# Attention scores by pairs of query tiles, with the low keys' product on 64 of the array's 128 rows

## The chip, the cores and the metric

The kernel runs on one core of one Trainium2 chip. The metric is the device time of one execution in microseconds (us), as the median of several runs. TensorE is called PE below, its weight loads PEld, VectorE DVE, ScalarE ACT, GpSimd POOL; the queues that issue their DMAs have a q behind the name.

## The reference

One layer of a hybrid decoder, with 2048 prompt rows and 8 sample rows. The change is inside branch A, causal attention over the prompt with 8 heads of width 64 and a decay term in the logits:

```python
def block(i):                       # 128 queries at a time, i = 0 .. 15
    qb = lax.dynamic_slice_in_dim(q, i * 128, 128, axis=1)
    cq = lax.dynamic_slice_in_dim(c, i * 128, 128, axis=2)
    sc = einsum('bqhd,bkhd->bhqk', qb, k) * 64 ** -0.5 + cq[..., None] - c[:, :, None, :]
    sc = where(kpos <= qpos, sc, -inf)
    p = softmax(sc, axis=-1)
    return einsum('bhqk,bkhd->bqhd', p, v)
```

The other branches (a gated recurrence, and cross-attention into 256 memory tokens), the input projection of 1024 columns into all of them, and the merge are left as they are.

## The kernel before

The program is a chain of stages on one core: the input rows are normalised and projected (to 903 us), the recurrence runs (925 to 1337 us), then the attention of branch A in `attend_prompt` (scores from 1382.7 to 2168.7 us), the memory attention (from 2218.4 us), and the merge, to 2859 us. PE works through the remaining columns of the input projection in the recurrence and both attentions: `fill` hands it a fixed number of such products at fixed places (L2683, 128x512 each), so that PE has work while other engines prepare the next attention step. How many there are, and where, is dealt out ahead by `fill.deal`, not by time.

All products keep about fp32 precision with two fp32r parts of each operand, a high one (hi) and the rest (lo). For the scores the two parts of the queries share one 128-row operand: `q_both` has q_hi in partitions 0 to 63 and q_lo in 64 to 127, and the keys are there twice, in both halves of `k_hi` and of `k_lo`. One 128-row product with `k_hi` (L399) so gives q_hi k_hi + q_lo k_hi; a second with `k_lo` (L400) adds q_hi k_lo + q_lo k_lo. A third product adds the causal mask on the 128 diagonal columns (L403).

One head has 16 query tiles of 128 rows (i), in four quads of four (q). The scores of a tile are made in chunks (c) of up to 512 keys, `CHUNKS[i] = i // 4 + 1` of them. A `("score", h, i, c)` step makes one chunk on PE in one of two PSUM banks (`S_BANKS = 2`), and DVE then adds the bias, takes the running maximum and puts the chunk into `probs` (L504), which frees the bank. After a tile's last chunk DVE reduces the maximum (L511) and ACT takes the exponential of the whole row (L454, the `exp` step). A `("key", h, q, j)` step turns the probabilities of four tiles against one block of 128 keys (up to four 128x128 transposes, L411), ACT and DVE split them into hi and lo (L463, L518), and PE multiplies those of two keys earlier by the values (L365). Each `key` step also holds two `fill` slots, of about 2.2 products each; the last one of a quad holds 7.5 (`SEAM`).

The order is written out ahead in one list, `steps`, that all engines walk. The scores of the next quad (`ahead`) are put among the key steps of this one: `some` is what falls to key j, spread over the first 80% of the quad's keys, or for the first quad of the next head at the keys in `NEXT_AT`. The `exp` steps (`late`) come behind the key step that follows the tile's last chunk. The first key step of a quad waits for all four of its exponentials (`exp_ready`). Each engine runs its own instructions strictly in this order.

The lines that matter for the score step on PE are:

```python
pe.matmul(out, q_both[:, i * P:(i + 1) * P], k_hi[:, keys], start=True, stop=False)        # L399
last = pe.matmul(out, q_both[:, i * P:(i + 1) * P], k_lo[:, keys], start=False, ...)       # L400
```

Of the kernel before, what the change touches and what calls it, by code (L numbers as in the profile page):

```python
# [18 lines left out]
P = 128  # L19
# [85 lines left out]
def attend_prompt(nc, core, block, queries, fox_k, fox_v, z_fox, neg_c, gated, fill, matmuls, first_matmuls, last_matmuls, recur, needed):  # L105
# [9 lines left out]
    DEPTH = 2  # L115
    AREA = [0, 24 * P * 2, 0, 24 * P * 2]
    PROBS = AREA[QUADS - 1] + 4 * T
    QUERIES_AT, KEYS_AT, VALUES_AT, NEXT_AT = (0, 3, 6, 9), (1, 4, 7, 10), (1, 4, 7, 10), (8, 10, 12, 14)
    quads = [(h, q) for h in range(FH) for q in range(QUADS)]

    steps = [("open", 0), ("fill", 0), ("open", 1), ("fill", 1), ("open", 2)] + [("queries", 0, b) for b in range(QUADS)]
    for b in range(QUADS):
        steps += [("keys", 0, b), ("fill", 2 + b)]
    steps += [("values", 0, b) for b in range(QUADS)]
    for i in range(4):
        steps += [("score", 0, i, 0), ("fill", 2 + QUADS + i), ("exp", 0, i)]
    FILLS = 2 + QUADS + 4
    for n, (h, q) in enumerate(quads):
        ahead = []
        if n + 1 < len(quads):  # L130
            g, p = quads[n + 1]
            ahead = [("score", g, i, c) for i in range(4 * p, 4 * p + 4) for c in range(CHUNKS[i])]
        keys = 4 * (q + 1)
        spread = max(1, round(keys * SPREAD))
        late = []
        for j in range(keys):
            if q == QUADS - 1:
                some = [st for st, at in zip(ahead, NEXT_AT) if at == j]
                if ahead and j in QUERIES_AT:
                    steps += [("queries", h + 1, QUERIES_AT.index(j))]  # L140
                if ahead and j in KEYS_AT:
                    steps += [("keys", h + 1, KEYS_AT.index(j))]
            else:
                if q == QUADS - 2 and h + 1 < FH and j in VALUES_AT:
                    steps += [("values", h + 1, VALUES_AT.index(j))]
                some = ahead[len(ahead) * min(j, spread) // spread:len(ahead) * min(j + 1, spread) // spread]
            steps += some
            steps += [("key", h, q, j)]
            steps += late
            late = [("exp", st[1], st[2]) for st in some if st[3] == CHUNKS[st[2]] - 1]  # L150
            if j == DEPTH - 1 and n > 0:
                steps += [("out", *quads[n - 1])]
            if j == DEPTH + 1 and n > 0:
                steps += [("back", *quads[n - 1])]
        steps += late
# [7 lines left out]
    with ExitStack() as ctx:  # L163
# [41 lines left out]
        def sem(name):  # L205
            return core.sem(f"fox_{name}")
# [12 lines left out]
        multiplied = sem("multiplied")  # L219
        o_copied, rows_ready = sem("o_copied"), sem("rows_ready")  # L220
        started, inverse_ready, halves_added = sem("started"), sem("inverse_ready"), sem("halves_added")

        def slots_of(st):

# [56 lines left out]
        def sync_steps(sp, some):  # L281
            with nc.allow_non_contiguous_dma(reason="a head's 64 columns of a row"):
                for st in some:
                    if st == ("open", 0):
                        recur.computed(sp)
                        fill.wait_stored(sp, needed)
                        for b in range(QUADS):
                            load_queries(sp, 0, b)
                        for n in range(2):
                            load_keys(sp, *quads[n])  # L290
                    if st == ("open", 1):
                        recur.store_state(sp)
# [12 lines left out]
                    if st == ("score", 0, 0, 0):  # L305
                        for n in range(QUADS, QUADS + 2):
                            load_queries(sp, *quads[n])
                            load_values(sp, *quads[n])
                    if st[0] == "keys" and quad_at[st[1], st[2]] + 2 < len(quads):
                        load_keys(sp, *quads[quad_at[st[1], st[2]] + 2])  # L310
                    if st[0] == "score" and st[2] == NT - 1 and st[3] == CHUNKS[-1] - 1 and st[1] + 1 < FH:
                        load_bias(sp, st[1] + 1)
                    if st[0] == "key":
                        for slot in slots_of(st):
                            fill.sync(sp, slot)
                    if st[0] == "back":
                        if quad_at[st[1], st[2]] + 2 < len(quads):
                            load_z(sp, *quads[quad_at[st[1], st[2]] + 2])
                        store(sp, st[1], st[2])
# [34 lines left out]
        def _(pe):  # L354
# [18 lines left out]
            for st in steps:  # L373
# [13 lines left out]
                if kind == "score":  # L387
                    i, c = rest
                    if (h, i, c) == (0, 0, 0):
                        pe.wait_ge(consts_ready, 1)  # L390
                    if i % 4 == 0 and c == 0:
                        pe.wait_ge(q_ready, h * QUADS + i // 4 + 1)
                        pe.wait_ge(turned_used, turn_at["keys", h, i // 4] + 1)
                    s = h * S_HEAD + S_AT[i] + c
                    if s >= S_BANKS:
                        pe.wait_ge(scores_used, s - S_BANKS + 1)
                    width = min(BANK, (i + 1) * P - c * BANK)
                    out, keys = scores[s % S_BANKS][:, 0:width], slice(c * BANK, c * BANK + width)
                    pe.matmul(out, q_both[:, i * P:(i + 1) * P], k_hi[:, keys], start=True, stop=False)  # L399
                    last = pe.matmul(out, q_both[:, i * P:(i + 1) * P], k_lo[:, keys], start=False,  # L400
                                     stop=c < CHUNKS[i] - 1)
                    if c == CHUNKS[i] - 1:
                        last = pe.matmul(out[:, width - P:width], ident_r[:], mask_r[:], start=False, stop=True)  # L403
                    last.then_inc(scored, 1)
                if kind == "key":
                    q, j = rest
                    if j == 0:
# [67 lines left out]
        def _(dve):  # L475
            for st in steps:
                kind, h, *rest = st
                if kind == "queries":
                    dve.wait_ge(q_hi_ready, h * QUADS + rest[0] + 1)
                    part = slice(rest[0] * BANK, (rest[0] + 1) * BANK)  # L480
                    dve.tensor_tensor(q_both[FD:P, part], raw_queries(h, rest[0])[FD:P, :], q_both[FD:P, part].bitcast(F32),
                                      ALU.subtract).then_inc(q_ready, 1)
                if kind == "values":
                    dve.wait_ge(v_hi_ready, h * QUADS + rest[0] + 1)
                    part = slice(rest[0] * 4, rest[0] * 4 + 4)
# [7 lines left out]
                                      ALU.subtract).then_inc(turned_used, 1)  # L493
                if kind == "score":
                    i, c = rest
                    slot = i // 4 % 2 * 4 + i % 4
                    if i == 0:
                        dve.wait_ge(bias_loaded, 16 * (h + 1))
                    if (h, i) == (0, 0):
                        recur.all_stored(dve)  # L500
                    s = h * S_HEAD + S_AT[i] + c
                    dve.wait_ge(scored, s + 1)
                    width = min(BANK, (i + 1) * P - c * BANK)
                    dve.tensor_tensor_reduce(probs_of(i, c * BANK, c * BANK + width), scores[s % S_BANKS][:, 0:width],  # L504
                                             bias[:, c * BANK:c * BANK + width], 1.0, NEG, ALU.add, ALU.max,
                                             most[:, slot, c:c + 1]).then_inc(scores_used, 1)
                    if c < CHUNKS[i] - 1:
                        continue

                    dve.wait_ge(scores_used, s + 1)  # L510
                    dve.tensor_reduce(neg_most[:, slot:slot + 1], most[:, slot, 0:CHUNKS[i]], AX.X, ALU.max,  # L511
                                      negate=True).then_inc(most_ready, 1)
                if kind == "key":
                    q, j = rest
                    zeta, skip = h * J_HEAD + J_AT[q] + j, max(0, j - 4 * q) * P
# [3008 lines left out]
```

## Time and profile before

| | |
|---|---|
| three runs | 2863.13 us median (2859.93 to 2865.31) |
| the profiled execution | 2860.77 us, of which the span of the trace is 2859.0 us |
| PE busy | 2742.8 us, 96% of the span |
| PE weight loads | 2247.4 us, 79% |
| DVE, ACT, POOL busy | 56%, 36%, 26% |
| granted TensorE clock, mean | 0.987 |

Two readings of a PE row need care. The duration of a matmul in the trace holds its whole passage through the array, so one of 512 columns shows 0.39 us, while the next starts 0.23 us after it: what it costs PE is the distance between starts. And a weight load has a row of its own (PEld, LDWEIGHTS) that normally lies beneath the matmul before it. In a row's form, `8*128 8x64` is a stationary operand of 8 rows and 128 columns and a moving one of 8 rows and 64 columns.

### The profile page before, as it was taken

Reading aid. Unit: us, or ns where it says so; the run is one execution under the profiler, and the core shown is the slowest. Engines: PE = TensorE matmul, PEld = TensorE weight load, DVE = VectorE, ACT = ScalarE, POOL = GpSimd, SP = SyncE. Lnnn points to the kernel's source line nnn. Section 1 sums busy time; section 2 is a strip of 40 time slices with the busy share of each in tenths; the row PEclk is TensorE's granted clock in tenths of the full one; section 3 lists DMA queues with packets and bytes.
Section 4 is the critical chain, followed back from the end, with each engine's and each line's share of the span. In section 5 each row is a group of like instructions: output and inputs, shape, how many; then the busy total and the mean of one; then the engine's idle time right before and its main releaser. Section 6 shows DMA issues by size and latency. Waiting matters only on the chain.

```text
span 2859.0 us, 38361 instructions
## 1 busy us (share of the span) xinstructions
PE 2742.8 (96%) x13712; PEld 2247.4 (79%) x13712; DVE 1596.8 (56%) x3067; ACT 1029.0 (36%) x1952; POOL 750.8 (26%) x688
## 2 busy tenths in 40 slices
PE   7999999999999999998899999999999998999998
PEld 6778777777778878787788788878778877888886
DVE  7424577543343676775466566656654754554545
ACT  2211111433322444452355455545543332322322
POOL 5148775044235352532020050020020232000000
PEclk9999999999999999999999999999999999999999
DMA  5677778667547666756654475455445564333331
GB/s 184 254 257 229 229 242 303 207 181 196 184 150 253 219 222 211 229 194 206 204 181 144 135 225 179 136 178 167 129 137 182 197 227 156 107 125 104 121 119 55
DMA packets 292075, 525.96 MB, mean 184 GB/s; under 512 B 111486, under 2 KB 120255, under 8 KB 270639
## 3 DMA queue, kind: packets, MB, share of 16 engines
q1 hardware_dynamic: 233247, 314.60, 35.6%
q10 hardware_dynamic: 56880, 204.34, 20.6%
q0 software_dynamic: 1760, 4.59, 0.4%
q8 instruction: 109, 1.79, 0.3%
q14 instruction: 79, 0.65, 0.1%
HBM read 411.02 MB, written 112.41 MB: 183 GB/s over the span
## 4 chain that ended last, share of the span: by engine, by line
PE 73%; POOL 6%; DVE 5%; DMA 4%; issue 3%; SPq 2%; ACT 1%; ACTq 0%; DVEq 0%; POOLq 0%
PE fill_out L2683 23%; PE fox_o_sum L365 4%; PE fox_turned L411 4%; PE in_out L100 4%; PE in_out L101 4%; PE in_out L102 4%; PE mf_out L100 3%; PE mf_out L101 3%; PE mf_out L102 3%; POOL dc_slot L1687 3%; PE fox_scores L399 2%; PE mf_fin L100 2%; PE mf_fin L102 2%; PE mf_fin L101 2%; PE fox_scores L400 2%
## 5 line engine op out<-in xcount | busy, mean ns | idle before, releaser
L2683 PE MATMUL fill_out<-keep_hi,fill_x 128*128 128x512 f32 x1488 | 513.6, 408 | 5.6 <-POOL keep_lo L2793 3.8
L2683 PEld LDWEIGHTS fill_out<-keep_hi,fill_x 128*128 128x128 f32 x1488 | 273.0, 190 | 54.1 <-POOL keep_lo L2793 5.3
L2683 PE MATMUL fill_out<-keep_lo,fill_x 128*128 128x512 f32 x744 | 302.9, 407 | 0.0
L518 DVE TENSOR_TENSOR fox_pt_lo<-fox_turned,fox_pt_hi 128x512 fp32r<-128x512 f32 (+1 forms) x320 | 194.9, 609 | 159.7 <-ACT fox_pt_hi L463 157.2
L463 ACT ACTIVATE fox_pt_hi<-fox_turned 128x512 fp32r<-128x512 f32 (+1 forms) x320 | 170.5, 533 | 304.2 <-PE fox_turned L411 301.4
L2277 ACT ACTIVATE in_stage<-in_out 128x512 f32<-128x512 f32 (+1 forms) x119 | 71.0, 598 | 554.9 <-PE in_out L102 522.7
L2784 POOL CAST keep_hi<-fill_raw 128x512 fp32r<-128x512 f32 x72 | 48.5, 673 | 723.0 <-PE fill_out L2693 700.5
L504 DVE CUSTOM_DVE_ANT_0 fox_probs<-fox_scores,fox_bias 128x512 f32<-128x512 f32 (+2 forms) x320 | 187.2, 607 | 89.8 <-PE fox_scores L400 58.8
L2683 PE MATMUL fill_out<-keep_hi,hg_fill_x 128*128 128x512 f32 x624 | 216.0, 408 | 6.8 <-POOL keep_lo L2793 5.4
L411 PE MATMUL fox_turned<-ident,fox_probs 128*128 128x128 f32 x1088 | 172.4, 274 | 8.4 <-ACT fox_probs L454 7.4
L2683 PEld LDWEIGHTS fill_out<-keep_lo,fill_x 128*128 128x128 f32 x744 | 141.5, 190 | 22.6
L411 PEld LDWEIGHTS fox_turned<-ident,fox_probs 128*128 128x128 f32 x1088 | 129.1, 141 | 36.5 <-ACT fox_probs L454 10.5
L454 ACT ACTIVATE fox_probs<-fox_probs,fox_neg_most 128x128 f32<-128x128 f32 (+15 forms) x128 | 153.3, 1198 | 10.6 <-ACT fill_stage L2709 9.7
L1687 POOL TENSOR_TENSOR dc_slot<-dc_slot,dc_q 128x1024 f32<-128x1024 f32 x54 | 135.3, 2511 | 65.1 <-DMA dc_slot<-in_cache_fox_k_dram 42.8
L2683 PEld LDWEIGHTS fill_out<-keep_hi,hg_fill_x 128*128 128x128 f32 x624 | 114.3, 190 | 26.5 <-POOL keep_lo L2793 5.8
L399 PE MATMUL fox_scores<-fox_k_hi,fox_q_both 128*128 128x512 f32 (+2 forms) x320 | 122.8, 384 | 11.7 <-DVE fox_most L504 10.2
L2709 ACT ACTIVATE fill_stage<-fill_out 128x512 f32<-128x512 f32 (+1 forms) x140 | 83.3, 595 | 137.7 <-PE fill_out L2683 126.3
L2683 PE MATMUL fill_out<-keep_lo,hg_fill_x 128*128 128x512 f32 x312 | 128.0, 410 | 0.0
L365 PE MATMUL fox_o_sum<-fox_pt_lo,fox_v_both 128*128 128x512 f32 (+1 forms) x320 | 116.6, 365 | 0.0
L365 PE MATMUL fox_o_sum<-fox_pt_hi,fox_v_both 128*128 128x512 f32 (+1 forms) x320 | 115.4, 361 | 0.3 <-ACT fox_o_turned L472 0.2
L100 PE MATMUL in_out<-x_first,rest_hi 128*128 128x512 f32 x288 | 112.6, 391 | 2.8 <-POOL rest_lo L2206 2.8
L100 PE MATMUL in_out<-rest_hi,x_first 128*128 128x512 f32 x288 | 115.1, 400 | 0.0
(420 smaller groups left out, 6752.7 us busy)
## 6 DMA issues: line engine op xcount, KB each, us to landing
fill_x<-x_tiles ACTq DMA_DIRECT2D x91, 1024.0 KB, 6.0
hg_fill_x<-x_tiles ACTq DMA_DIRECT2D x38, 1024.0 KB, 5.4
dc_slot<-in_cache_fox_k_dram SPq DMA_DIRECT2D x128, 256.0 KB, 3.7
dc_slot<-in_cache_fox_v_dram SPq DMA_DIRECT2D x128, 256.0 KB, 3.5
in_raw<-in_w_in_dram SPq DMA_DIRECT2D x104, 256.0 KB, 4.2
plain<-fill_stage ACTq DMA_DIRECT2D x96, 256.0 KB, 5.1
turned<-in_stage ACTq DMA_DIRECT2D x64, 256.0 KB, 3.9
fill_raw<-in_w_in_dram SPq DMA_DIRECT2D x56, 256.0 KB, 2.8
```

Of the source, the lines that this page charges most:

```text
L100: pe.matmul(out, a[0], b[0], start=first, stop=False)
L101: pe.matmul(out, a[1], b[0], start=False, stop=False)
L102: return pe.matmul(out, a[0], b[1], start=False, stop=last)
L365: last = pe.matmul(o_sum[:, skip:BANK], v_both[h % 2][:, j, :], p[:, zeta % PT_SLOTS, skip:BANK], start=(j == 0 and m == 0), stop=(j == 4 ...
L399: pe.matmul(out, q_both[:, i * P:(i + 1) * P], k_hi[:, keys], start=True, stop=False)
L411: last = pe.transpose(bank_of(st)[:, t * P:(t + 1) * P], probs_of(4 * q + t, j * P, (j + 1) * P), core.ident[:])
L454: act.activation(probs_of(i, 0, (i + 1) * P), probs_of(i, 0, (i + 1) * P), ACT.Exp, bias=neg_most[:, slot:slot + 1], accum_out=row_sum[:, ...
L463: act.activation(pt_hi[:, zeta % PT_SLOTS, skip:BANK], bank_of(st)[:, skip:BANK], ACT.Copy).then_inc(hi_ready, 1)
L504: dve.tensor_tensor_reduce(probs_of(i, c * BANK, c * BANK + width), scores[s % S_BANKS][:, 0:width], bias[:, c * BANK:c * BANK + width], 1 ...
L518: dve.tensor_tensor(pt_lo[:, b, skip:BANK], bank_of(st)[:, skip:BANK], pt_hi[:, b, skip:BANK].bitcast(F32), ALU.subtract).then_inc(turned_ ...
L1687: eng.tensor_tensor(slot, slot, self.q[r % self.QS][:].to_broadcast([P, self.GP, W]), ALU.mult).then_inc(signal, 1)
L2683: ins = pe.matmul(self.out[n % self.OUTS][:], x, w, start=(k == 0 and term == 0), stop=(ends and term == 2))
```

## The change

A score step now covers two tiles, i and i + 1, and makes chunk c of both, one in each PSUM bank. PE first makes both `k_hi` products (128 rows, with their masks), and then both `k_lo` products, each of 64 rows: the even tile's in partitions 0 to 63, the odd tile's in 64 to 127. In the program as built these carry the array position of 64 rows from row 0 and 64 rows from row 64. The product q_lo k_lo is no longer made. For the odd tile to have q_hi in the upper half, the subtraction that makes q_lo runs on the upper half for even tiles and on the lower half for odd ones (two DVE instructions of 64x2x128 for one of 64x512).

```diff
-    QUERIES_AT, KEYS_AT, VALUES_AT, NEXT_AT = (0, 3, 6, 9), (1, 4, 7, 10), (1, 4, 7, 10), (8, 10, 12, 14)
+    QUERIES_AT, KEYS_AT, VALUES_AT, NEXT_AT = (0, 3, 6, 9), (1, 4, 7, 10), (1, 4, 7, 10), (9, 13)
...
-            ahead = [("score", g, i, c) for i in range(4 * p, 4 * p + 4) for c in range(CHUNKS[i])]
+            ahead = [("score", g, i, c) for i in range(4 * p, 4 * p + 4, 2) for c in range(CHUNKS[i])]
...
-            steps += some
+            steps += some[:1]
             steps += [("key", h, q, j)]
+            steps += some[1:]
             steps += late
-            late = [("exp", st[1], st[2]) for st in some if st[3] == CHUNKS[st[2]] - 1]
+            late = [("exp", st[1], k) for st in some if st[3] == CHUNKS[st[2]] - 1 for k in (st[2], st[2] + 1)]
...
-                    s = h * S_HEAD + S_AT[i] + c
-                    if s >= S_BANKS:
-                        pe.wait_ge(scores_used, s - S_BANKS + 1)
-                    width = min(BANK, (i + 1) * P - c * BANK)
-                    out, keys = scores[s % S_BANKS][:, 0:width], slice(c * BANK, c * BANK + width)
-                    pe.matmul(out, q_both[:, i * P:(i + 1) * P], k_hi[:, keys], start=True, stop=False)
-                    last = pe.matmul(out, q_both[:, i * P:(i + 1) * P], k_lo[:, keys], start=False,
-                                     stop=c < CHUNKS[i] - 1)
-                    if c == CHUNKS[i] - 1:
-                        last = pe.matmul(out[:, width - P:width], ident_r[:], mask_r[:], start=False, stop=True)
-                    last.then_inc(scored, 1)
+                    parts = []
+                    for k in range(i, i + 2):
+                        s = score_at(h, k, c)
+                        if s >= S_BANKS:
+                            pe.wait_ge(scores_used, s - S_BANKS + 1)
+                        width = min(BANK, (k + 1) * P - c * BANK)
+                        out, keys = scores[s % S_BANKS][:, 0:width], slice(c * BANK, c * BANK + width)
+                        pe.matmul(out, q_both[:, k * P:(k + 1) * P], k_hi[:, keys], start=True, stop=False)
+                        if c == CHUNKS[k] - 1:
+                            pe.matmul(out[:, width - P:width], ident_r[:], mask_r[:], start=False, stop=False)
+                        parts.append((out, keys))
+                    for k, (out, keys) in zip((i, i + 1), parts):
+                        half = slice(k % 2 * FD, k % 2 * FD + FD)
+                        pe.matmul(out, q_both[half, k * P:(k + 1) * P], k_lo[half, keys], start=False, stop=True
+                                  ).then_inc(scored, 1)
...
-                    dve.tensor_tensor(q_both[FD:P, part], raw_queries(h, rest[0])[FD:P, :], q_both[FD:P, part].bitcast(F32),
-                                      ALU.subtract).then_inc(q_ready, 1)
+                    for odd, half in enumerate((slice(FD, P), slice(0, FD))):
+                        lo = q_both[half, part].rearrange("p (n o c) -> p n o c", o=2, c=P)[:, :, odd, :]
+                        raw = raw_queries(h, rest[0])[half, :].rearrange("p (n o c) -> p n o c", o=2, c=P)[:, :, odd, :]
+                        last = dve.tensor_tensor(lo, raw, lo.bitcast(F32), ALU.subtract)
+                    last.then_inc(q_ready, 1)
```

On DVE a score step now runs L504's work for both tiles, each behind its own wait on `scored`, and after the last chunk both reductions of the maximum; `score_at` numbers the chunks so that the even tile's are in bank 0 and the odd tile's in bank 1.

On PE, the scores of quad 1 among the key steps of quad 0 in the first head show the new order of products. `turned` rows are a key step's transposes, x3 and x2 of them for keys 1 and 2. Before, behind key 0:

```order
L399 MATMUL fox_scores1<-fox_k_hi,fox_q_both 128x384
L400 MATMUL fox_scores1<-fox_k_lo,fox_q_both 128x384
L403 MATMUL fox_scores1<-fox_mask_r,fox_ident_r 128x128
L399 MATMUL fox_scores0<-fox_k_hi,fox_q_both 128x512
L400 MATMUL fox_scores0<-fox_k_lo,fox_q_both 128x512
L399 MATMUL fox_scores1<-fox_k_hi,fox_q_both 128x512
L400 MATMUL fox_scores1<-fox_k_lo,fox_q_both 128x512
L403 MATMUL fox_scores1<-fox_mask_r,fox_ident_r 128x128
L411 MATMUL fox_turned0<-ident,fox_probs 128x128 x2
```

These are the last three chunks of quad 1, all ahead of key 2. In the change the same place, with key 2 and what lies between it and key 3:

```order
L408 MATMUL fox_scores0<-fox_k_hi,fox_q_both 128x512
L408 MATMUL fox_scores1<-fox_k_hi,fox_q_both 128x512
L414 MATMUL fox_scores0<-fox_k_lo,fox_q_both 128x512
L414 MATMUL fox_scores1<-fox_k_lo,fox_q_both 128x512
L422 MATMUL fox_turned0<-ident,fox_probs 128x128 x2
...
L408 MATMUL fox_scores0<-fox_k_hi,fox_q_both 128x384
L410 MATMUL fox_scores0<-fox_mask_r,fox_ident_r 128x128
L408 MATMUL fox_scores1<-fox_k_hi,fox_q_both 128x512
L410 MATMUL fox_scores1<-fox_mask_r,fox_ident_r 128x128
L414 MATMUL fox_scores0<-fox_k_lo,fox_q_both 128x384
L414 MATMUL fox_scores1<-fox_k_lo,fox_q_both 128x512
L422 MATMUL fox_turned1<-ident,fox_probs 128x128
```

The two `k_lo` products of a pair (L414) now stand together, between products of 128 rows; and the quad's last pair stands behind key 2 where its last chunks stood ahead of it.

## Rows read from the trace of the kernel before

**Rows 1.** The page: the chain that ended last, by engine.

```profile
PE 73%; POOL 6%; DVE 5%; DMA 4%; issue 3%; SPq 2%; ACT 1%; ACTq 0%; DVEq 0%; POOLq 0%
```

**Rows 2.** Busy time by engine over eight windows of 100 us, 1380 to 2180.

```profile
sum 800.00, PE 778.60 PEld 643.49 DVE 492.66 ACT 411.12 POOL 91.99; mean PE 97.32 PEld 80.44 DVE 61.58 ACT 51.39 POOL 11.50
```

**Rows 3.** What PE waited for in 1375 to 2185: total us, times, longest.

```profile
PE fox_scores L399 <- DVE fox_most L504: 10.2, 21, 1.6
PE fox_turned L411 <- ACT fox_probs L454: 7.4, 7, 1.6
```

**Rows 4.** Groups by form: the products with `k_lo` of 512 columns.

```profile
L400 PE MATMUL fox_scores<-fox_k_lo,fox_q_both 128*128 128x512 f32 x224 | 87.9, 392 | 0.0
```

**Rows 5.** Timeline of PE: start, duration, line; around 1500 us.

```profile
1500.99 0.39 PE L399 MATMUL fox_scores<-fox_k_hi,fox_q_both 128*128 128x512 f32 x1
1501.22 0.39 PE L400 MATMUL fox_scores<-fox_k_lo,fox_q_both 128*128 128x512 f32 x1
...
1501.50 0.28 PE L400 MATMUL fox_scores<-fox_k_lo,fox_q_both 128*128 128x128 f32 x1
1501.62 0.28 PE L403 MATMUL fox_scores<-fox_mask_r,fox_ident_r 128*128 128x128 f32 x1
...
1506.81 0.34 PE L399 MATMUL fox_scores<-fox_k_hi,fox_q_both 128*128 128x384 f32 x1
1506.99 0.35 PE L400 MATMUL fox_scores<-fox_k_lo,fox_q_both 128*128 128x384 f32 x1
```

**Rows 6.** Timeline, 523.1 to 524.2: an 8-row product among 128-row ones.

```profile
523.19 0.39 PE L102 MATMUL in_out<-rest_lo,x_first 128*128 128x512 f32 x1
523.50 0.29 PEld L1836 LDWEIGHTS in_small<-dc_spread,dc_ones 8*128 8x128 f32 x2 [0.35 <-issue]
523.51 0.40 PE L1836 MATMUL in_small<-dc_spread,dc_ones 8*128 8x32 f32 x2
...
523.84 0.45 PE L1859 MATMUL in_wide<-keep_hi,dc_pr 128*66 128x512 f32 x1
```

**Rows 7.** The instructions that make the operand of that product.

```profile
L1774 DVE TENSOR_TENSOR dc_spread<-ident,dc_bias x2: 178/196/214, 485.8 to 514.8; 8x64 f32<-8x64 f32 x1, 8x32 f32<-8x32 f32 x1
```

**Rows 8.** Timeline, 650.4 to 651.3: a small product of all 128 rows.

```profile
650.54 0.40 PE L102 MATMUL in_out<-x_first,keep_hi 128*128 128x512 f32 x1
650.54 0.42 PEld L1973 LDWEIGHTS in_small<-sr_part,ff_before 128*128 128x128 f32 x2
650.77 0.28 PE L1973 MATMUL in_small<-sr_part,ff_before 128*128 128x1 f32 x2
...
650.91 0.43 PE L1859 MATMUL in_wide<-keep_hi,dc_pr 128*66 128x512 f32 x1
```

**Rows 9.** Timeline, 486.0 to 487.1: the other 8-row product.

```profile
486.01 0.39 PE L102 MATMUL in_out<-rest_lo,x_first 128*128 128x512 f32 x1
...
486.69 0.50 PE L100 MATMUL in_out<-rest_hi,x_first 128*128 128x512 f32 x1
...
487.02 0.40 PE L101 MATMUL in_out<-rest_hi,x_first 128*128 128x512 f32 x1
```

**Rows 10.** The second weight load of that product, in a window of its own.

```profile
486.43 0.18 PEld L1836 LDWEIGHTS in_small<-dc_spread,dc_ones 8*128 8x128 f32 x1
```

**Rows 11.** Timeline at the seam from quad 0 to 1, head 1.

```profile
1508.89 0.69 DVE L504 CUSTOM_DVE_ANT_0 fox_probs<-fox_scores,fox_bias 128x512 f32<-128x512 f32 x1
...
1510.32 0.27 PE L411 MATMUL fox_turned<-ident,fox_probs 128*128 128x128 f32 x1
...
1510.80 1.04 ACT L454 ACTIVATE fox_probs<-fox_probs,fox_neg_most 128x896 f32<-128x896 f32 x1
```

**Rows 12.** The end of that seam, timeline 1512.8 to 1515.

```profile
1512.86 0.19 ACT L454 ACTIVATION_READ_ACCUMULATOR fox_probs<-fox_probs,fox_neg_most 128x1 f32 x1
...
1514.46 0.60 PE L411 MATMUL fox_turned<-ident,fox_probs 128*128 128x128 f32 x4
```

**Rows 13.** The subtraction that makes q_lo, on DVE.

```profile
L481 DVE TENSOR_TENSOR fox_q_both<-fox_q_raw,fox_q_both x28: 689/690/1830, 1465.8 to 2092.6; 64x512 fp32r<-64x512 f32 x28
```

More of the change, by code:

```diff
@@ L124, in attend_prompt @@
     steps += [("values", 0, b) for b in range(QUADS)]
-    for i in range(4):
-        steps += [("score", 0, i, 0), ("fill", 2 + QUADS + i), ("exp", 0, i)]
+    for i in range(0, 4, 2):
+        steps += [("score", 0, i, 0)]
+        for k in range(i, i + 2):
+            steps += [("fill", 2 + QUADS + k), ("exp", 0, k)]
     FILLS = 2 + QUADS + 4
@@ L221, in attend_prompt, with score_at @@
         started, inverse_ready, halves_added = sem("started"), sem("inverse_ready"), sem("halves_added")
+        def score_at(h, i, c):
+            return h * S_HEAD + S_AT[i - i % 2] + 2 * c + i % 2
         def slots_of(st):
@@ L310, in sync_steps @@
                         load_keys(sp, *quads[quad_at[st[1], st[2]] + 2])
-                    if st[0] == "score" and st[2] == NT - 1 and st[3] == CHUNKS[-1] - 1 and st[1] + 1 < FH:
+                    if st[0] == "score" and st[2] == NT - 2 and st[3] == CHUNKS[-1] - 1 and st[1] + 1 < FH:
                         load_bias(sp, st[1] + 1)
@@ L393, in _ @@
                         pe.wait_ge(turned_used, turn_at["keys", h, i // 4] + 1)
-                    s = h * S_HEAD + S_AT[i] + c
-                    if s >= S_BANKS:
-                        pe.wait_ge(scores_used, s - S_BANKS + 1)
-                    width = min(BANK, (i + 1) * P - c * BANK)
-                    out, keys = scores[s % S_BANKS][:, 0:width], slice(c * BANK, c * BANK + width)
-                    pe.matmul(out, q_both[:, i * P:(i + 1) * P], k_hi[:, keys], start=True, stop=False)
-                    last = pe.matmul(out, q_both[:, i * P:(i + 1) * P], k_lo[:, keys], start=False,
-                                     stop=c < CHUNKS[i] - 1)
-                    if c == CHUNKS[i] - 1:
-                        last = pe.matmul(out[:, width - P:width], ident_r[:], mask_r[:], start=False, stop=True)
-                    last.then_inc(scored, 1)
+                    parts = []
+                    for k in range(i, i + 2):
+                        s = score_at(h, k, c)
[11 more added lines that the diff above has]
+                                  ).then_inc(scored, 1)
                 if kind == "key":
@@ L495, in _ @@
                     i, c = rest
-                    slot = i // 4 % 2 * 4 + i % 4
                     if i == 0:
@@ L500, in _ @@
                         recur.all_stored(dve)
[L501 to L506, printed above, removed]
+                    for k in range(i, i + 2):
+                        slot, s = k // 4 % 2 * 4 + k % 4, score_at(h, k, c)
+                        dve.wait_ge(scored, s + 1)
+                        width = min(BANK, (k + 1) * P - c * BANK)
+                        dve.tensor_tensor_reduce(probs_of(k, c * BANK, c * BANK + width), scores[s % S_BANKS][:, 0:width],
+                                                 bias[:, c * BANK:c * BANK + width], 1.0, NEG, ALU.add, ALU.max,
+                                                 most[:, slot, c:c + 1]).then_inc(scores_used, 1)
                     if c < CHUNKS[i] - 1:
                         continue
-                    dve.wait_ge(scores_used, s + 1)
-                    dve.tensor_reduce(neg_most[:, slot:slot + 1], most[:, slot, 0:CHUNKS[i]], AX.X, ALU.max,
-                                      negate=True).then_inc(most_ready, 1)
+                    for k in range(i, i + 2):
+                        slot = k // 4 % 2 * 4 + k % 4
+                        dve.wait_ge(scores_used, score_at(h, k, c) + 1)
+                        dve.tensor_reduce(neg_most[:, slot:slot + 1], most[:, slot, 0:CHUNKS[k]], AX.X, ALU.max,
+                                          negate=True).then_inc(most_ready, 1)
                 if kind == "key":
```

## The prediction

> **What bounds the kernel now.** I began with the chain that ended last: PE makes 73% of it, no other engine more than 6% [rows 1]. The question is whether this holds in the stage that the change touches. The table of windows says so: from 1380 to 2180 PE is busy 97.3% of the time, DVE 61.6%, ACT 51.4% [rows 2]. The waits give the small rest: in some 810 us PE waited 10.2 us for DVE to free a score bank, in 21 places, and 7.4 us for exponentials, in 7 [rows 3]. So in this stage time is what PE's instructions need, and as the fill products are dealt out by count, whatever PE saves or loses per score step goes straight into the total. POOL, DMA and the later stages follow on PE's end of this stage and do not shorten or hide it.
>
> The duration of a score product (392 ns in its group, [rows 4]) is not its price. The timeline gives that as the distance between starts: 0.23 us for 512 columns, 0.18 for 384, 0.12 for 128 [rows 5]. 256 columns lie between the last two; I take 0.12.
>
> **The saving on paper.** A head has 20 pairs: 12 in which both chunks have 512 columns, and 8 that end their tiles, with 384 and 512 columns or 128 and 256, four of each. Over 8 heads that is 96, 32 and 32 pairs. If the two `k_lo` products ran side by side and nothing else changed, each pair would save the shorter one: 96 x 0.23 + 32 x 0.18 + 32 x 0.12 = 31.7 us.
>
> **What a visit to part of the rows costs.** The trace has no 64-row product, but it has two places where one product of 8 rows (issued as two pairs of load and matmul) stands among 128-row ones. In ordinary work the next weights are loaded beneath the matmul before. The control is a small 128-row product: its first weight load starts at 650.54, together with the matmul ahead of it, and the row of 128-row work behind it starts 0.37 us after that matmul [rows 8]. The 8-row product is different: the matmul ahead starts at 523.19, and its first weight load only at 523.50, 0.31 later [rows 6]. That is 0.23 for the matmul's columns and some 0.08 more. It was not waiting for data: its operand was made at 514.8 plus 0.2 us, over 8 us earlier [rows 7], and the trace puts the gap down to no releaser. The next 128-row weights also start only when the 8-row products are through, 0.65 us after the matmul ahead, against 0.37 in the control. The other place repeats it: 0.68 us from 486.01 to 486.69, with 64 moving columns where this one had 32, and then 0.33 instead of 0.23 to the next start, since the first weights of the return are not hidden [rows 9]. So PE empties on the way in and on the way out, and no weight load is hidden across either border.
>
> From this a pair of two full chunks, counted from the start of its second `k_hi` product to the moment at which ordinary spacing resumes. The visit of [rows 9] took 0.68; its last matmul had 64 columns, about 0.06 of it (32 columns more made a difference of 0.03 between the two visits); now it has 512, 0.23: 0.68 - 0.06 + 0.23 = 0.85. It already holds two weight loads one behind the other, 0.11 apart (486.43 against 486.32) [rows 10]; with the second half starting 0.11 behind the first, the two streams overlap for the rest. The exposed load on return adds 0.10: 0.95 us. Before, the same stretch was three spacings, 0.69. **A full pair costs 0.26 more.**
>
> A pair of 384 and 512 with masks: before 2 x 0.18 + 2 x 0.23 + 2 x 0.12 = 1.06. After: 0.18 + 0.12 + 0.23, then the visit counted from a mask of 128 columns, 0.95 - 0.17 = 0.78, sum 1.31: 0.25 more. A pair of 128 and 256: before 6 x 0.12 = 0.72; after 3 x 0.12, and 0.78 - 0.11 for the shorter stream, 1.03: 0.31 more. Sum: 96 x 0.26 + 32 x 0.25 + 32 x 0.31 = **+43 us**.
>
> Bounds of what no row shows. If the two halves load their weights at the same time, 0.11 less in each of 160 pairs: +25. If the two streams do not overlap, the odd one waits for the even one instead of starting 0.11 behind: 0.12 more in 96 pairs, 0.06 in 32: +56. I take the serial loads with overlapping streams, since the two loads of the 8-row visit, the nearest row, came 0.11 apart.
>
> The Trainium skill has a rule for this middle case. Its page "TensorE: Matmul & The Clock Gate", section "Part 3 — Packing small matmuls — row/col tiling", has matmuls on different row groups start about 4 ns apart, with weight loads overlapping. No product here uses two row groups, so the trace can't say. By that rule the two loads hide each other, and the sum would be the lower bound, +25.
>
> **The other parts.** Waits for a bank: 10.2 us [rows 3] came where two or three chunks stood in a row, each needing DVE's 0.69 us [rows 11] for the one two before. A pair now has both banks and then at least one key step (four transposes, five fill products and two value products, about 2 us) before the next pair; DVE needs about 1.5 us for a pair. I give back 8 of the 10.2.
>
> The seam of quad 0: the last pair is now made behind key 2, not ahead of it. In head 1 before, key 3's transpose stands at 1510.32 and the next quad's first key, which needs all exponentials, at 1514.46, 4.14 us later; ACT had ended the last exponential at 1512.86 + 0.19, 1.4 us early [rows 11, 12]. After: from the pair's end DVE needs at most 2 x 0.69 for the two chunks, and an estimated 0.5 for two reductions and the signals; then ACT makes two exponentials, which took 2.25 from 1510.80 to that end: 4.1 us in all. PE's cover is 4.14 plus 0.26 for the pair behind the seam. That is just covered, and where ACT has an eviction of a fill unit in its queue PE waits. Behind the waiting transpose stand the key step's fill and all later work. Eight such seams at 0.5 us: +4. Elsewhere two exponentials now stand back to back in ACT's queue; three banks for turned rows and values two key steps behind leave PE some 4 us to go on, so I cost this at nothing; without that cover the 24 other quads could lose about 0.5 us each.
>
> DVE makes q_lo in two instructions instead of one of 690 ns [rows 13]. Even if each cost 0.5 us, 32 x 0.3 = 10 us of DVE lie in a stage in which it is idle 38% of the time; cost zero. Issue counts of PE, DMA and fill stay the same.
>
> Total: +43 - 8 + 4 = +39 us. Against the profiled execution's 2860.8 that is 2900; the median of the runs is 2.3 us above it, so **2902 us**, 1.4% slower. What a measurement can tell from no change is about 0.2%, 6 us.
>
> **Rivals.**
>
> A, no emptying (faster). The delay in [rows 6, 9] would belong to the 8-row product (its fp32 form, its semaphore wait) and not to part-row work as such. The control speaks against it: it is fp32 too, and has a wait too. If PE pulls both half loads beneath the second `k_hi` product, the gain is 31.7 us; if the second load still shows, 0.11 x 160 = 17.6 less. With -4 from the waits: 2827 to 2845. The sign turns where both borders and the bare loads together cost a full pair less than the 0.23 it saves; [rows 6, 8] show 0.28 more for a tiny product.
>
> In the Trainium skill, "TensorEngine Tiling (Array Packing)", section "Key Properties", says that changing the tiling mode drains TensorE, which is against A; the 0.31 us of [rows 6] agree. But the page of the clock gate, section "Part 3 — Packing small matmuls — row/col tiling", has the weight load for another row group pulled ahead of running matmuls. That would be A's way, and our 8-row load did not do it behind a full-height matmul.
>
> B, loads side by side: 2863 + 25 - 4 = 2884. For it: separate halves; against: the only loads in a row here are serial.
>
> C, streams not side by side: 2863 + 56 - 4 = 2915. For it: no row here shows two streams at once. Against: only that the halves write different banks and read different partitions.
>
> D, exponentials late in each quad, on top of the forecast: 8 seams at the longest wait of before, 1.6 us [rows 3], and 24 at 0.5 are 25 us, less the 4 counted: 2923. It decides nothing of the sign.
>
> E, emptying one way only: with the return load beneath the streams, 0.08 of emptying and 0.10 of load fall away, 29 us in 160 pairs. From the forecast that leaves 2873, from B 2855: about no change, 2864.
>
> **How the numbers follow.** Forecast (serial loads, streams together) 0.45; B 0.20; C 0.12; D 0.03; A 0.14; E 0.06. Slower by over 0.2% is the first four, 0.80; within it 0.06; faster 0.14. The forecast's own range, from spacings read to 0.01 us and the seam, is 2888 to 2915. For 8 in 10 it must take B and C: down to 2868, below B, where E's dearer form lies, and up to 2928, past D. That leaves out A and half of E, and little above.
>
> **What would show it.** In the changed trace the first half-row weight load starts 0.3 us after the last 128-row matmul of the pair (A: at its start), the second about 0.11 behind the first (B: at the same time); the two L414 matmuls 0.11 apart (C: 0.23); the next 128-row start about 0.85 us after the second `k_hi` product. The stage from the first score to the last grows by about 39 us, PE's waits for DVE at the scores fall to 2 us or less, waits for exponentials stay below 12 us, and stages outside do not move. The prediction is wrong if half-row weights lie beneath the full-height matmul, which turns the sign, or if PE's waits for ACT grow beyond 20 us.

## The result: 0.66% slower, and the profile after

The changed kernel took 2880.17 us (median of 4 runs, 2877.55 to 2884.45), the kernel before 2862.32 beside it. The ratio is 1.0066, with a 95% interval of 1.0052 to 1.0080. The sign of the prediction held, and the time lies in its widest range (2868 to 2928), but below the 2888 to 2915 of its own case: of the 39 us that it gave, less than half came, 18 us. They came in the stage that was changed. From the first `k_hi` product to the last it is 804.4 us (1380.3 to 2184.7) in place of 785.6 (1382.7 to 2168.3), 19 us more.

The page of the changed kernel gives the busy times and the chain that ended last:

```profile
span 2875.9 us, 38393 instructions
...
PE 2765.7 (96%) x13712; PEld 2215.0 (77%) x13712; DVE 1582.5 (55%) x3099; ACT 1029.4 (36%) x1952; POOL 750.8 (26%) x688
...
PE 71%; POOL 6%; DMA 5%; DVE 4%; issue 3%; ACT 3%; SPq 3%; ACTq 0%; POOLq 0%; DVEq 0%
```

PE is still what bounds it, and ACT has a larger share of the chain than before (3% against 1%, [rows 1]). The list of waits of PE from 1375 to 2205 us (total, times, longest) answers to [rows 3]:

```profile
PE fox_turned L422 <- ACT fox_probs L465: 8.0, 14, 2.5
PE fill_out L2699 <- ACT fill_stage L2725: 2.8, 3, 2.4
PE fox_scores L408 <- DVE fox_most L518: 1.9, 3, 0.8
```

The waits for a bank fell from 10.2 to 1.9 us, as forecast. Those for exponentials hardly grew in total, but they now have single ones of 2.5 us, and a new one of 2.4 us for an eviction. The eviction meant here is ACT's copy of a finished fill unit out of its bank (L2725). One pair of full chunks, in the timeline around 1511 us:

```profile
1510.58 0.71 PE L408 MATMUL fox_scores<-fox_k_hi,fox_q_both 128*128 128x512 f32 x2
...
1511.22 0.19 PEld L414 LDWEIGHTS fox_scores<-fox_k_lo,fox_q_both 64*128 64x128 f32 x2 [0.36 <-issue]
1511.22 0.50 PE L414 MATMUL fox_scores<-fox_k_lo,fox_q_both 64*128 64x512 f32 x2
...
1511.64 0.42 PEld L422 LDWEIGHTS fox_turned<-ident,fox_probs 128*128 128x128 f32 x4 [0.24 <-issue]
1511.65 0.66 PE L422 MATMUL fox_turned<-ident,fox_probs 128*128 128x128 f32 x4
...
1512.06 0.48 PE L2699 MATMUL fill_out<-keep_lo,hg_fill_x 128*128 128x512 f32 x1
```

The border on the way in is there: the half-row weights begin only when the 128-row products are through, and PEld sat idle for 0.36 us with no releaser but "issue". The border on the way out is there too, with 0.24 us. What is different from the forecast is between them: the row holds two weight loads (x2) and is 0.19 us long, the length of one. The two halves load at the same time, both matmuls fit into 0.50 us, and from their start to the next 128-row start it is 0.43 us.

### The profile page after: what moved, and what is told of

Same layout as the page of the kernel before. It is cut to its first block, busy times and chain, and to the rows that moved or that the text cites. A ratio compares the mean times of both kernels' runs of the same rounds, so it can differ in the third digit from the quotient of the medians.

```text
span 2875.9 us, 38393 instructions
## 1 busy us (share of the span) xinstructions
PE 2765.7 (96%) x13712; PEld 2215.0 (77%) x13712; DVE 1582.5 (55%) x3099; ACT 1029.4 (36%) x1952; POOL 750.8 (26%) x688
## 4 chain that ended last, share of the span: by engine, by line
PE 71%; POOL 6%; DMA 5%; DVE 4%; issue 3%; ACT 3%; SPq 3%; ACTq 0%; POOLq 0%; DVEq 0%
PE fill_out L2699 22%; PE fox_turned L422 5%; PE fox_o_sum L372 4%; PE in_out L100 4%; PE in_out L101 4%; PE in_out L102 4%; PE mf_out L100 3%; PE mf_out L101 3%; PE mf_out L102 3%; POOL dc_slot L1703 2%; PE fox_scores L408 2%; PE fox_scores L414 2%; PE mf_fin L100 2%; PE mf_fin L102 2%; PE mf_fin L101 2%
## 5 line engine op out<-in xcount | busy, mean ns | idle before, releaser
L422 PE MATMUL fox_turned<-ident,fox_probs 128*128 128x128 f32 x1088 | 180.8, 282 | 9.0 <-ACT fox_probs L465 8.0
L2725 ACT ACTIVATE fill_stage<-fill_out 128x512 f32<-128x512 f32 (+1 forms) x140 | 83.3, 595 | 131.9 <-PE fill_out L2699 120.1
L100 PE MATMUL in_out<-rest_hi,x_first 128*128 128x512 f32 x288 | 114.4, 397 | 0.4 <-DVE in_stage L2324 0.4
L101 PE MATMUL in_out<-rest_hi,x_first 128*128 128x512 f32 x288 | 113.4, 394 | 0.0
```

The source lines that it names most:

```text
L100: pe.matmul(out, a[0], b[0], start=first, stop=False)
L101: pe.matmul(out, a[1], b[0], start=False, stop=False)
L422: last = pe.transpose(bank_of(st)[:, t * P:(t + 1) * P], probs_of(4 * q + t, j * P, (j + 1) * P), core.ident[:])
L2725: act.activation(self.stage[n % self.STAGES][0:rows, :], self.out[n % self.OUTS][0:rows, :], ACT.Copy).then_inc(self.taken, 1)
```

## The experiments

**Full rows, order of pairs kept.** Only the height of the low-key products goes back to 128 rows:

```diff
-                        half = slice(k % 2 * FD, k % 2 * FD + FD)
+                        half = slice(0, P)
```

> The change with its order of steps, but each low-key product contracts all 128 rows again (so q_lo k_lo is computed again). No border between 128-row and 64-row work is left. Theory (the borders cost about 20 us, and the order of pairs alone is worth the bank waits less the late exponentials): close to the kernel before, 2855 to 2864 us, PE's waits for a score bank near 2 us. Rival (the order itself is what costs, by seams and stalls, and the borders are nearly free): stays within 4 us of the change, 2876 or more.

It took 2862.05 us, ratio to the kernel before 1.0002 (0.9993 to 1.0011). So the 64-row products with their borders (the two changes between 128-row and 64-row work around each pair) cost 2880.2 - 2862.1 = 18 us, and all the rest of the change together costs nothing: the theory's 2855 to 2864 holds and the rival falls. That nothing is a balance of parts, as the later runs show. Its timeline shows the same place of a pair without borders:

```profile
1508.01 0.63 PE L414 MATMUL fox_scores<-fox_k_lo,fox_q_both 128*128 128x512 f32 x2
1508.48 0.60 PE L422 MATMUL fox_turned<-ident,fox_probs 128*128 128x128 f32 x4
1508.84 0.48 PE L2699 MATMUL fill_out<-keep_lo,hg_fill_x 128*128 128x512 f32 x1
```

Two full-row products take 0.47 to the first transpose, and the four transposes 0.36. In the change they take 0.43 and 0.41: 0.04 less and 0.05 more. So the streams side by side save 0.04 against two in a row, and the return gives it back. What remains is the way in: from the first `k_hi` product to the half-row ones it is 0.55 where no transposes stand ahead of the pair (0.64 above, where they do), and two spacings are 0.46. In the changed kernel's timeline:

```profile
1519.56 0.61 PE L408 MATMUL fox_scores<-fox_k_hi,fox_q_both 128*128 128x512 f32 x2
1520.11 0.50 PE L414 MATMUL fox_scores<-fox_k_lo,fox_q_both 64*128 64x512 f32 x2
```

Together 0.10 us for a full pair, or 16 us if all 160 pairs cost as much.

**No low-key products.** The loop that makes them is taken out, and `scored` is incremented behind the high product or its mask.

> The change without any low-key product: the 320 products are left out, so the scores lack q_hi k_lo. Theory (the stage is bound by PE): against the version with full rows it saves 224 x 0.23 + 32 x 0.18 + 64 x 0.12 = 65 us, less about 8 for the exposed waits that a shorter PE no longer covers: 2790 to 2806 us. Rival (ACT and DVE are close behind PE, and the paired exponentials bind first): saves less than 45 us, 2815 or more.

It took 2820.44 us (ratio 0.9854, 0.9839 to 0.9869): 42 us less than with full rows, where PE has 65 us less to do. The theory gave 2790 to 2806 and is wrong, the rival's 2815 or more holds. The waits of PE in the stage show what takes up the rest:

```profile
PE fox_scores L408 <- DVE fox_most L514: 13.9, 20, 2.8
PE fox_turned L418 <- ACT fox_probs L461: 10.5, 14, 2.5
```

Against 2.9 and 8.2 us with full rows these are 13 us more, and the granted clock, 1.00 in all eight windows of 100 us with full rows, is 0.97 or 0.98 in five, which sums to 12 us lost. Together that is about the 23 us by which the saving fell short. So, in this order of steps, even a version whose low keys cost nothing would have gained under 1.5%; the cover for DVE and ACT in this stage is thin.

**Both low-key products in the same half.**

```diff
-                        half = slice(k % 2 * FD, k % 2 * FD + FD)
+                        half = slice(0, FD)
...
-                    for odd, half in enumerate((slice(FD, P), slice(0, FD))):
+                    for odd, half in enumerate((slice(FD, P), slice(FD, P))):
```

> The change with both low-key products of a pair in rows 0 to 63 (the even and the odd tile have q_hi below), so the borders stay and only the side-by-side running goes. Theory (in the change the two halves run side by side in full): each pair loses the shorter stream again, 96 x 0.23 + 32 x 0.18 + 32 x 0.12 = 32 us, 2905 to 2915 us. Rival (the second stream was hidden only in part, starting one weight load behind): 96 x 0.12 + 32 x 0.07, 2892 to 2896 us. Rival (no overlap in the change): same as the change, 2880.

It took 2904.98 us (ratio 1.0153, 1.0137 to 1.0168), 25 us above the change. The first row is its weight loads, the others its PE, in the two timelines from 1500 us:

```profile
1507.26 0.29 PEld L414 LDWEIGHTS fox_scores<-fox_k_lo,fox_q_both 64*128 64x128 f32 x2 [0.35 <-issue]
```

```profile
1507.26 0.73 PE L414 MATMUL fox_scores<-fox_k_lo,fox_q_both 64*128 64x512 f32 x2
1507.92 0.66 PE L422 MATMUL fox_turned<-ident,fox_probs 128*128 128x128 f32 x4
```

Here the loads are 0.11 apart (0.29 for two), and the next 128-row work follows after 0.66 us, not 0.43: 0.23 more, a whole stream. The total stands at the lower end of the theory's 2905 to 2915. It fell short of the 32 us by 7 and lies above the 16 us of a partly hidden stream; the row decides for streams that ran fully side by side in the change. Part of the shortfall is seen: the waits for exponentials are 6.7 us in place of 8.0, and the stage has one fall of the clock, 1.7 us, in place of two (below). The other 4 us stay open.

**Even tile only.** The odd tile's low-key product is left out; the even one increments `scored` by 2, behind both high products.

> The change without the odd tile's low-key product (left out: 160 products of 64 rows, so the odd tiles' scores lack q_hi k_lo). Theory (the odd stream lies wholly beside the even one, its weights too): 96 full pairs cost the same, 64 pairs end 0.05 us earlier with the even tile's shorter stream: 2875 to 2881 us. Rival (the second product starts one weight load behind): 160 x 0.11 = 18 us less, 2862. Rival (they run one after the other): 32 us less, 2848.

2879.05 us (ratio 1.0056, 1.0040 to 1.0071), 1 us from the change, within the theory's 2875 to 2881. The odd product costs nothing beside the even one:

```profile
1506.89 0.50 PE L416 MATMUL fox_scores<-fox_k_lo,fox_q_both 64*128 64x512 f32 x1
1507.32 0.66 PE L424 MATMUL fox_turned<-ident,fox_probs 128*128 128x128 f32 x4
```

One product or two, the next start comes 0.43 us later. Both rivals (2862 and 2848) fall.

**Single tiles, 64 rows.** The kernel before, with `q_both[0:FD, ...]` and `k_lo[0:FD, keys]` in L400.

> The kernel before with its own order, single tiles, but each low-key product over rows 0 to 63 alone. So 320 visits to 64-row work with nothing beside them. Theory (each visit costs two borders: 0.33 in, 0.43 to the next 128-row weight load, 0.06 of exposed load, against 0.46 for two full-row products): 0.36 x 320 = 115 us, less some 8 of bank waits, 2955 to 2975 us. Rival (a border costs only when two halves are addressed in turn, not for the change of height): within 20 us of the kernel before.

2956.88 us (ratio 1.0323, 1.0308 to 1.0339). So 320 visits with nothing beside them cost 93 us; with the 10 us by which its waits for banks fell (to 0.5), 0.32 us each, and 0.33 if the 3.6 us are added by which its waits for exponentials fell (7.4 to 3.8). That is within the theory's 2955 to 2975, and the rival falls. In its timeline:

```profile
1508.08 0.39 PE L399 MATMUL fox_scores<-fox_k_hi,fox_q_both 128*128 128x512 f32 x1
1508.40 0.50 PE L400 MATMUL fox_scores<-fox_k_lo,fox_q_both 64*128 64x512 f32 x1
1508.83 0.33 PE L403 MATMUL fox_scores<-fox_mask_r,fox_ident_r 128*128 128x128 f32 x1
```

0.32 in and 0.43 out, against 0.23 each: 0.09 and 0.20 more. The border belongs to the change of height, not to the use of two halves.

**Exponentials apart.**

```diff
             steps += late
-            late = [("exp", st[1], k) for st in some if st[3] == CHUNKS[st[2]] - 1 for k in (st[2], st[2] + 1)]
+            steps += [("exp", st[1], st[2]) for st in some[:1] if st[3] == CHUNKS[st[2]] - 1]
+            late = [("exp", st[1], st[2] + 1) for st in some[:1] if st[3] == CHUNKS[st[2]] - 1]
+            late += [("exp", st[1], k) for st in some[1:] if st[3] == CHUNKS[st[2]] - 1 for k in (st[2], st[2] + 1)]
```

> The change, but where a pair is completed ahead of a key step, the even tile's exponential follows that key step and the odd tile's the next one, instead of both in a row one key step later. Theory (two stalls of PE of 2.4 us behind two long exponentials, each with a fall of the granted clock to 0.5 for some 3 us, cost about 8 us of the change's loss): 2871 to 2876 us, no fall of the clock within the stage. Rival (the stalls only move, or ACT now waits for DVE in front of an exponential and holds up the next copy): 2878 or more.

2869.99 us (ratio 1.0032, 1.0020 to 1.0043), 10 us below the change, 1 us below the theory's 2871 to 2876; the rival falls. Why, is seen in the changed kernel's timeline at a seam from quad 2 to 3:

```profile
1665.36 1.89 ACT L465 ACTIVATE fox_probs<-fox_probs,fox_neg_most 128x1920 f32<-128x1920 f32 x1
...
1667.24 1.99 ACT L465 ACTIVATE fox_probs<-fox_probs,fox_neg_most 128x2048 f32<-128x2048 f32 x1
...
1669.38 0.59 ACT L2725 ACTIVATE fill_stage<-fill_out 128x512 f32<-128x512 f32 x1
...
1670.03 1.22 PE L2699 MATMUL fill_out<-keep_hi,hg_fill_x 128*128 128x512 f32 x2 [2.44 <-ACT fill_stage L2725]
```

Two exponentials of a pair stand in a row, 4 us of ACT, and the eviction of a fill unit behind them: the fill products, which should have covered the seam, themselves wait 2.44 us for a bank. At the same seam two heads later there is a second such stall, but there PE waits for the exponential itself:

```profile
1880.96 0.66 PE L422 MATMUL fox_turned<-ident,fox_probs 128*128 128x128 f32 x4 [2.49 <-ACT fox_probs L465]
```

Such a stall can cost twice. Windows of 2 us around the first (the granted clock is the third number from the end):

```profile
1668.00:1670.00 2.00, 0.00 (x0) 0.00 (x0) 0.29 (x1) 1.98 (x4) 1.65 (x2) 0.98 1.09 345
1670.00:1672.00 2.00, 1.97 (x5) 1.60 (x6) 0.00 (x0) 1.17 (x2) 0.00 (x0) 0.50 1.05 365
1672.00:1674.00 2.00, 2.00 (x10) 1.56 (x9) 0.84 (x2) 0.15 (x2) 0.00 (x0) 0.66 0.91 336
1674.00:1676.00 2.00, 2.00 (x16) 1.78 (x15) 0.69 (x1) 0.99 (x2) 0.00 (x0) 1.00 0.67 234
```

After it the clock was granted at 0.50, the lower of its two levels (1.2 and 2.4 GHz), and lost 1.7 us more. It happened twice in this trace, at 1670 and 1882. With the exponentials apart, waits for them fell from 8.0 to 2.2 us, and in the trace of that run no window of 10 us between 1390 and 2160 has a lower clock. 5.8 + 0.6 (evictions) + 3.4 (clock) is 9.8 of the 10.2 us. The sum sets single profiled executions, whose stage (first to last `k_hi` product) is 12.7 us shorter, against medians, so it fits only roughly, and its clock part is the least sure. The next run has the same order of exponentials; its trace has a wait of 1.85 us for an eviction at the same seam, at 1669.7, and the clock falls behind it all the same (0.83 in the window from 1670 to 1680). The version with full rows and paired exponentials had both stalls (2.45 and 2.48 us) and no fall.

**Full rows and exponentials apart.** Both edits above.

> Pairs of tiles and exponentials apart, as in the run before with that name, but each low-key product over all 128 rows: the borders go, the rest stays. Theory (borders 18 us, paired exponentials 10 us, both independent): the full-row version at 2862 less 10, so 2850 to 2856 us, faster than the kernel before by 0.2 to 0.4%. Rival (with the shorter PE stage the stalls come back elsewhere, as they did without low-key products): 2859 or more.

2851.66 us (ratio 0.9961, 0.9947 to 0.9975): faster than the kernel before by 0.4%, within the theory's 2850 to 2856, and 10.4 us below full rows alone. The two costs, borders and paired exponentials, add up.

**The same, each tile's products in turn.** The step still covers two tiles, but its products stand as high, low, mask for the even tile, then for the odd, with `scored` incremented behind each tile.

> Steps by pairs and exponentials apart, full-row products, and within a pair each tile's products one after the other (high, low, mask, then the odd tile), as the kernel before makes them, where the run before this one had both high products first. Theory (only the order of steps and exponentials gives the gain; the even tile's bank is now ready for DVE 0.35 us sooner): 2849 to 2855 us, same as that run. Rival (the order of products within the pair had a share in the gain): 2857 or more.

2846.22 us (ratio 0.9941, 0.9927 to 0.9955), the fastest of all. It is 3 us below the theory's band, and the rival, by which the time would rise to 2857 or more, had the wrong direction. The order within the pair has a share of its own, a gain of about 5 us: the two intervals overlap a little, but each of the six runs is faster than each of the five with both high products first. The first rows are from the timeline with both high products first:

```profile
1530.72 0.69 DVE L520 CUSTOM_DVE_ANT_0 fox_probs<-fox_scores,fox_bias 128x512 f32<-128x512 f32 x1
...
1531.16 0.22 PE L412 MATMUL fox_scores<-fox_mask_r,fox_ident_r 128*128 128x128 f32 x1
...
1531.47 0.50 PE L410 MATMUL fox_scores<-fox_k_hi,fox_q_both 128*128 128x512 f32 x1
```

and these, of the same work, with the products in turn:

```profile
1524.42 0.69 DVE L517 CUSTOM_DVE_ANT_0 fox_probs<-fox_scores,fox_bias 128x512 f32<-128x512 f32 x1
...
1525.03 0.22 PE L413 MATMUL fox_scores<-fox_mask_r,fox_ident_r 128*128 128x128 f32 x1
...
1525.17 0.50 PE L409 MATMUL fox_scores<-fox_k_hi,fox_q_both 128*128 128x512 f32 x1
```

From the even tile's mask to the odd tile's high product it is 0.31 against 0.14. In both places the product starts 0.06 us after DVE has read the odd bank's last chunk (to 1531.41 and 1525.11). In the early order PE comes to that bank one low product sooner and stands longer. The lists of PEld's waits for banks in the stage, again the early order first, agree:

```profile
PEld fox_scores L410 <- DVE fox_most L520: 16.4, 34, 1.4
```

```profile
PEld fox_scores L409 <- DVE fox_most L517: 11.4, 21, 1.4
```

Waits are not the whole of it. A masked pair takes less in turn even where nothing is waited for: from its first product to the next work 0.63 us, not 0.68, for 128 and 256 columns, and 0.99, not 1.05, for 384 and 512. Over 64 such pairs that is 3 to 4 us, of which the next weight loads take back about one. No run separates the two parts. The change has the early order too, since its two `k_lo` products stand side by side behind both high ones.

## Why the prediction went wrong in size

**What held.** PE bounds the stage. It empties on the way into half-height work and out of it, with 0.32 us to the first 64-row load, where the 8-row products had shown 0.31 [rows 6]. The bank waits gave back 8.3 us, where I had 8. So the sign and its reason were right. One reading was weaker than I wrote: at the second 8-row place [rows 9] the trace does name a releaser, DVE's operand, though that was ready at 486.04, 0.28 us before the load. The 64-row products show the same delay with no releaser but "issue".

**The step that failed: the price of a visit, +43 us.** I chose serial weight loads, "since the two loads of the 8-row visit, the nearest row, came 0.11 apart". Those two loads went to the same rows of the array. With both products in one half they are 0.11 apart again, and in two halves they start together. The nearest row was near in height and wrong in the one respect that mattered. This is 0.11 in 160 pairs, 18 us too much: rival B, with +25, had the price. By the runs it is 18 us against full rows in the new order of products. The term was counted against the old order, and against that the rows below give 22 us, where I had 43. The rule of the Trainium skill that I had set beside it ("TensorE: Matmul & The Clock Gate", Part 3, on row groups) agrees: two loads took 0.19 us, and the second stream cost nothing.

**Two smaller errors in the same term.** The return costs 0.05 us of exposed load, not 0.10, which is 8 us in 160 pairs; mostly transposes stand behind it. The other error has the opposite sign, 5 us in 64 pairs: I set what a masked pair took before too high, 1.06 and 0.72. The fastest kernel above makes these products in the old order, and its timeline shows 0.99 from the pair of 384 and 512 to the next work, and 0.63 for 128 and 256:

```profile
1501.30 0.22 PE L409 MATMUL fox_scores<-fox_k_hi,fox_q_both 128*128 128x128 f32 x1
...
1501.93 0.51 PE L421 MATMUL fox_turned<-ident,fox_probs 128*128 128x128 f32 x3
1502.19 0.48 PE L2698 MATMUL fill_out<-keep_lo,hg_fill_x 128*128 128x512 f32 x1
...
1505.95 0.34 PE L409 MATMUL fox_scores<-fox_k_hi,fox_q_both 128*128 128x384 f32 x1
...
1506.94 0.28 PE L421 MATMUL fox_turned<-ident,fox_probs 128*128 128x128 f32 x1
1506.98 0.48 PE L2698 MATMUL fill_out<-keep_hi,hg_fill_x 128*128 128x512 f32 x1
```

In the changed kernel the same two places take 0.81 and 1.10 us, and the transposes behind them 0.04 more each:

```profile
1501.28 0.23 PE L408 MATMUL fox_scores<-fox_k_hi,fox_q_both 128*128 128x128 f32 x1
...
1502.09 0.55 PE L422 MATMUL fox_turned<-ident,fox_probs 128*128 128x128 f32 x3
1502.39 0.48 PE L2699 MATMUL fill_out<-keep_lo,hg_fill_x 128*128 128x512 f32 x1
...
1506.28 0.34 PE L408 MATMUL fox_scores<-fox_k_hi,fox_q_both 128*128 128x384 f32 x1
...
1507.38 0.33 PE L422 MATMUL fox_turned<-ident,fox_probs 128*128 128x128 f32 x1
1507.46 0.49 PE L2699 MATMUL fill_out<-keep_hi,hg_fill_x 128*128 128x512 f32 x1
```

So a pair of 128 and 256 costs 0.22 us more than in the old order (I had 0.31), one of 384 and 512 costs 0.15 (I had 0.25), and a full pair about 0.11 (I had 0.26). The last is 1.39 us from the first `k_hi` product to the work behind the transposes (1519.56 to 1520.95), against 1.28 in the full-row run (1516.16 to 1517.44), whose products take the same for such a pair in either order. So the term is 32 x 0.22 + 32 x 0.15 + 96 x 0.11 = 22 us. The three errors account for it: 43 - 18 - 8 + 5 = 22.

**The seams.** I costed two exponentials in a row at nothing and named the seam of quad 0, at +4. The seam that cost most was that from quad 2 to 3, with two stalls of 2.4 and 2.5 us: one by a path that I had not drawn, the eviction behind the exponentials and the fill behind the eviction, the other by the exponential itself. All paired exponentials together cost about 10 us by the run without them, of which PE's own lists of waits show 6. In the total it went unseen: in the full-row version, which landed on 1.0002, what the pair steps gave back hid it.

**The balance of the change**, by the runs: borders +18; paired exponentials +10; the order of products within a pair about +5; and against these the pair steps themselves, which with full rows, exponentials apart and products in turn gain 17 us. Of these 17 the lists of PEld's waits, before and in the fastest kernel, show where most may lie: for banks 26.0 and 11.4 us, for exponentials 10.5 and 5.0. No run separates them. In the prediction's own terms the visits cost 22 or 23 us where it had 43, the pair steps gave back 17 where it had 8, and the exponentials cost 10 where it had 4. The last two errors nearly cancel, which was luck, so that what is left of the 39 us is off by about the error in the price of a visit.

## What to carry to other kernels

Cutting a product to half the array's rows pays only if the streams run side by side long enough to pay for both borders: here one saved stream of 0.23 us stood against emptying twice and bare loads, 0.33 us by the run with single tiles, and 18 us were lost over 160 visits. By these two figures, as an estimate, a visit would have to save at least two such streams; no run here made one that did. When one part of a change loses, run the rest without it: the pair steps, freed from the half rows and with their exponentials apart, were worth 0.4%, and 0.6% with each tile's products in turn. And when work is gathered into pairs, look at what the other engines now do twice in a row, and at what is queued behind it.

## What the runs showed of the hardware

Products on rows 0 to 63 and 64 to 127 that write different banks run fully side by side, weight loads included: two loads in 0.19 us and the next work after 0.43 us, with one product or with two. On the same rows the loads are 0.11 us apart and the streams follow one another (0.66 us).

A change from 128-row to 64-row work costs about 0.09 us (0.32 between starts, not 0.23), the change back about 0.20 (0.43, not 0.23), and the first weights on either side are not loaded beneath the work ahead of them. A visit with one product costs 0.33 us in all, as the mean of 320.

Waits of PE of 2.44 and 2.49 us were each followed by a granted clock of 0.50 for some 3 us in the changed kernel. Not every such wait is: with both low-key products in one half one of two was (2.43, not 2.48), in the full-row version neither (2.45 and 2.48), and of two shorter ones the 1.85 us with full rows and exponentials apart was, the 1.88 us with exponentials apart was not.
